# Two-layer hybrid encoder on 8 cores: casts of layer 1's mixer weights over eight steps from the fifth on, transfers of the weight sums on SyncE's queue, two of four query tiles evicted by VectorE

## The chip, the cores and the metric

The kernel runs on the 8 cores of one Trainium2 chip. Each core computes one of the 8 sequences of the batch, with the same program and the same weights; nothing passes between cores. The metric is the time on the device of the slowest core, in microseconds. The profile is that of one execution, taken on the slowest core.

## The reference

Two layers over x of shape (8, 4096, 1024), float32:

```python
for l in range(DEPTH):
    h = rmsnorm(x, norm1_g[l])
    q, k, v, r, fz, gb_in, gc_in, cx, ga, gb = split(h @ w_in[l])
    log_a = log_sigmoid(fz @ w_fg2[l] + b_fg[l]) / 16
    o = gla_chunk_causal(q * 128 ** -0.5, k, v, log_a)      # chunks of 64 frames, 4 heads
    y_a = (rmsnorm_per_head(o) * gla_norm_g[l] * silu(r)) @ w_oa[l]
    y_b = (gb_in * causal_depthwise_conv3(gc_in * cx)) @ w_ob[l]
    x = x + (sigmoid(ga) * y_a + sigmoid(gb) * y_b) @ w_o[l]
    h2 = rmsnorm(x, norm2_g[l])
    x = x + (silu(h2 @ w_gate[l]) * (h2 @ w_up[l])) @ w_down[l]   # hidden width 2816
return rmsnorm(x, final_g)
```

## The kernel before

**Steps.** A sequence of 4096 frames is cut into 8 tiles of 512. The program is a list of 24 steps: steps 0 to 7 are the mixer of layer 0 (one tile each), 8 to 11 the feed-forward part (FFN) of layer 0 (two tiles each), 12 to 19 the mixer of layer 1, 20 to 23 the FFN of layer 1. The FFN multiplies 2 by 2 blocks by Strassen's seven products, so it needs sums of weight blocks.

**Weights.** Every step streams all its weights as bf16 through a ring in SBUF (`wring`): four slots for the 20 mixer blocks of up to 1280 KB, five for FFN blocks (44 products' blocks of the gate and up weights come as 22 loads of 896 KB, `sc_gu`; 28 loads of 352 KB for the down weights, `sc_dn`). The next load is issued on SyncE's (SP's) queue by `done_block` when a slot comes free. The bf16 copies lie in DRAM and are made by the kernel itself:

- Layer 0's mixer weights are cast as they are first loaded, in steps 0 and 1, on GpSimd's (POOL's) queue.
- Layer 1's mixer weights are cast from DRAM to DRAM by 40 DMAs of `cast_piece` (L393), each half a block, issued from POOL's queue. Before: ten in each of steps 8 to 11.
- The FFN's weights of both layers go through `prep_jobs`: 66 pieces a layer. Each is loaded into `pin` (512 KB, `prep_load`, L399), POOL forms five sums and a copy in three jobs (`first`, `second`, `third`; L415 and L410), and `third` then issues the load of the next piece and the store of `pout` (448 KB, L433). Before, load and store are on POOL's queue. The pieces of layer 0 are spread over steps 2 to 7, those of layer 1 over steps 12 to 19. There is one `pin` and one `pout`, so `first` of the next piece waits until the store of this one has landed.

**Order.** Every engine runs its instructions in the order in which the program emits them. A step is a generator that yields after each group of matmuls (87 yields in a mixer step, 180 in an FFN step). After each yield the main loop also advances `sides` (norms, loads and stores of x) and pops jobs from the step's list, evenly over the yields. A job's `pace()`, and the like wait in `cast_piece`, hold POOL until TensorE (PE) has done what has been emitted so far. In a mixer step POOL also computes two small operations per unit of the linear attention, `rs2` (L751 and L753, in `C(u)`), which `E2(u)` on VectorE (DVE, L759) reads; the transposes of `Tr(u)` on PE (L768) follow.

**The start of a mixer step.** Block `fzq` gives the forget-gate code and the four query tiles in five PSUM banks. DVE copies the first (L665). The queries are scaled and evicted by ScalarE (ACT) (L674), two before and two after `gate1`, which puts eight ACT operations (four Exp, L632; four Ln, L635) between them. There are eight banks: the four groups of `v0` reuse the banks of the four queries.

Of the kernel before, what the change touches and what calls it, by code (L numbers as in the profile page):

```python
# [9 lines left out]
AF = mybir.ActivationFunctionType  # L10
ALU = mybir.AluOpType
# [24 lines left out]
class Trk:  # L36
# [56 lines left out]
    def op(self, en, R, W, f):  # L93
        e = self.E[en]
        self.deps(e, R, W)
        f(e.h).then_inc(e.sem, 1)
        e.cnt += 1
        self.record(R, W, (e.sem, e.cnt, en))
# [14 lines left out]
    def dma(self, qn, R, W, dsem, f):  # L113
        e = self.E[qn]
        self.deps(e, R, W)
        f(e.h).then_inc(dsem[0], 16)
        dsem[1] += 16
        self.record(R, W, (dsem[0], dsem[1], "dma"))
# [11 lines left out]
def _mixer_blocks():  # L130

    c = _cols()
    w = lambda n, o, k: ("w_in", c[n] + o, k)
    bl = [("fzq", 8, 640, [w("fz", 0, 16)] * 8 + [w("q", 0, 512)])]
    bl += [("v0", 8, 512, [w("v", 0, 512)])]
    bl += [("k", 8, 512, [w("k", 0, 512)])]
    bl += [("v1", 8, 512, [w("v", 512, 512)])]
    bl += [("r%d" % h, 8, 512, [w("r", h * 512, 512)]) for h in range(2)]
    bl += [("cv%d" % i, 8, 640, [w(n, i * 128, 128) for n in ("C", "X", "B", "ga", "gb")]) for i in range(8)]
    bl += [("%s%d" % (n[2:], h), 8, 512, [(n, h * 512, 512)]) for h in range(2) for n in ("w_ob", "w_oa")]  # L140
    bl += [("o%d" % h, 8, 512, [("w_o", h * 512, 512)]) for h in range(2)]
    return bl


def _ffn_blocks():

    bl = [("%s%d" % (n, p), 1, 28 * 128, None) for p in range(NPAIR) for n in ("g", "u")]
    return bl + [("d%d%s" % (n, m), 1, NPAIR * 128, None) for n in range(4) for m in PROD]
# [6 lines left out]
PH = [("mix", 0), ("ffn", 0), ("mix", 1), ("ffn", 1)]  # L155
BLOCKS = {"mix": _mixer_blocks(), "ffn": _ffn_blocks()}
# [3 lines left out]
def build_nc(S):  # L160
# [20 lines left out]
    def wblock(l, bi):  # L181
        o = sum(MIXSIZE[:bi])
        return wmix[l][o:o + MIXSIZE[bi]].rearrange("(p n) -> p n", p=128)

    with ExitStack() as es:
        tk = Trk(nc, es)
        op, mms, dma = tk.op, tk.mms, tk.dma
# [27 lines left out]
        def carve(shape, dt, mode, keys, split=False):  # L215
            n = int(np.prod(shape))
            w = n if dt == F32 else n // 2
            per = w // len(keys) if split else 0
            for i, k in enumerate(keys):
                span[k] = (mode, ao[0] + i * per, ao[0] + (i + 1) * per) if per else (mode, ao[0], ao[0] + w)  # L220
            v = (arena if dt == F32 else a16)[:, (ao[0] if dt == F32 else 2 * ao[0]):(ao[0] if dt == F32 else 2 * ao[0]) + n]
            ao[0] += w
            assert ao[0] <= AW, (mode, ao[0])
            if len(shape) == 2:
                v = v.rearrange("p (a b) -> p a b", a=shape[0])
            return v

        R2 = lambda n, a, b: [(n, i, j) for i in range(a) for j in range(b)]
        R1 = lambda n, a: [(n, i) for i in range(a)]

        qT = carve([4, T], BF16, "mix", R1("qT", 4), True)
# [12 lines left out]
        pin = carve([4, PIECE], F32, "mix", ["pin"])  # L244
        pout = carve([7, PIECE], BF16, "mix", R1("pout", 7), True)
# [43 lines left out]
        pb = [es.enter_context(nc.psum_tensor("pb%d" % i, [128, 512], F32)) for i in range(8)]  # L289
        BK = lambda i: ("bank", i)  # L290
# [5 lines left out]
        def bank():  # L296
            b = ring[0][ri[0] % len(ring[0])]
            ri[0] += 1
            return b
# [4 lines left out]
        steps = [(p, t) for p in range(4) for t in range(NT if PH[p][0] == "mix" else NT // 2)]  # L304
# [80 lines left out]
        def cast_piece(l, bi, hf):  # L385
            e = tk.E["pool"]
            tk.wait(e, tk.E["pe"].sem, tk.E["pe"].cnt)
            ds = psem[pcount[0] % NPS]
            pcount[0] += 1
            if ds[1]:  # L390
                tk.wait(e, ds[0], ds[1])
            dma("pool", [], [("scr", "mix", l, bi, hf)], ds,
                lambda q: q.dma_start(out=scr[("mix", l, bi)][64 * hf:64 * hf + 64, :], in_=wblock(l, bi)[64 * hf:64 * hf + 64, :]))  # L393

        pisem, posem = tk.newsem("pin"), tk.newsem("pout")

        def prep_load(l, i):
            dma("pool", [], ["pin"], pisem,
                lambda q: q.dma_start(out=pin, in_=wffn[l][i].rearrange("p (a b) -> p a b", a=4)))  # L399

        def prep_jobs(l):

            A12, A21, A22, A11 = (pin[:, j, :] for j in range(4))

            def pace():
                tk.wait(tk.E["pool"], tk.E["pe"].sem, tk.E["pe"].cnt)

            def total(nm, x, o, y):
                m = WSUM[nm]
                op("pool", ["pin"], [("pout", m)], lambda h: h.tensor_tensor(out=pout[:, m, :], in0=x, in1=y, op=o))  # L410

            def first():
                pace()
                op("pool", ["pin"], [("pout", 5), ("pout", 6)],
                   lambda h: h.tensor_copy(out=pout[:, 5:7, :], in_=pin[:, 2:4, :]))  # L415
                total("M1", A11, ALU.add, A22)

            def second():
                pace()
                total("M2", A21, ALU.add, A22)  # L420
                total("M5", A11, ALU.add, A12)

            def third(i):
                pace()
                total("M6", A21, ALU.subtract, A11)
                total("M7", A12, ALU.subtract, A22)
                if i + 1 < NPIECE:
                    prep_load(l, i + 1)
                if i < 2 * GQ:
                    dst = scr[("gu", l, i // 2)].rearrange("p (h a b) -> p h a b", h=2, a=7)[:, i % 2, :, :]  # L430
                else:
                    dst = scr[("dn", l)][:, :, (i - 2 * GQ) * PIECE:(i - 2 * GQ + 1) * PIECE]
                dma("pool", R1("pout", 7), [("prep", l, i)], posem, lambda q: q.dma_start(out=dst, in_=pout))  # L433

            yield lambda: prep_load(l, 0)
            for i in range(NPIECE):
                yield first
                yield second
                yield lambda i=i: third(i)
                for _ in range(5):  # L440
                    yield lambda: None
# [168 lines left out]
        def mixer(s):  # L610
            p, t = steps[s]
            l = PH[p][1]
# [54 lines left out]
            for hh in range(4):  # L667
                if hh == 2:
                    gate1()
                b = bs[1 + hh]  # L670
                if s:
                    fm_group(b, w, wk, 128 + hh * 128, h_, hk)
                op("act", [BK(b)], [("qT", hh), BK(b)],
                   lambda h, hh=hh, b=b: h.activation(out=qT[:, hh, :], in_=pb[b][:, :], func=AF.Copy, scale=128.0 ** -0.5))  # L674
                yield
            done_block(sl)

# [17 lines left out]
            for hh in range(4):  # L695
                b = bank()
                fm_group(b, w, wk, hh * 128, h_, hk)
                op("dve", [BK(b), ("dec", hh)], [("kdT", hh), BK(b)],
                   lambda h, b=b, hh=hh: h.tensor_tensor(out=kdT[:, hh, :], in0=pb[b][:, :], in1=dec[:, hh, :], op=ALU.mult))
# [182 lines left out]
            for i in range(4):  # L882
                b = bank()
# [227 lines left out]
        jobs = {}  # L1111

        def spread(fs, lo, hi):

            us = {"mix": 166.0, "ffn": 200.0}
            length = [us[PH[steps[s][0]][0]] for s in range(lo, hi)]
            ends = list(itertools.accumulate(length))
            for i, f in enumerate(fs):
                at = ends[-1] * i / len(fs)
                jobs.setdefault(lo + next(n for n, e_ in enumerate(ends) if at < e_), []).append(f)  # L1120

        NG = NT // 2
        F0, M1 = NT, NT + NG
        spread(list(prep_jobs(0)), 2, F0)
        spread([lambda bi=bi, hf=hf: cast_piece(1, bi, hf) for bi in range(len(BLOCKS["mix"])) for hf in range(2)], F0, M1)
        spread(list(prep_jobs(1)), M1, M1 + NT)

        def lead(n):
# [65 lines left out]

        GROUPS = {"mix": 87, "ffn": 180}
        RUN = {"mix": mixer, "ffn": ffn}
        for s, (p, t) in enumerate(steps):
            kind, l = PH[p]
            sg = sides(s)
            wst["kind"] = kind  # L1200
            issue_loads()
            todo = jobs.get(s, [])
            n, gi = len(todo), 0
            for _ in RUN[kind](s):
                gi += 1
                next(sg, None)
                while todo and gi * (n + 1) > GROUPS[kind] * (n - len(todo) + 1):
                    todo.pop(0)()
            for _ in sg:
                pass  # L1210
            while todo:
                todo.pop(0)()
# [79 lines left out]
```

How the kernel before makes its waits and increments, by code:

```python
    def wait(self, e, sem, val):  # L52
        if e.waited.get(id(sem), 0) < val:
            e.h.wait_ge(sem, val)
            e.waited[id(sem)] = val
# [37 lines left out]
    def op(self, en, R, W, f):  # L93
        e = self.E[en]
        self.deps(e, R, W)
        f(e.h).then_inc(e.sem, 1)
        e.cnt += 1
        self.record(R, W, (e.sem, e.cnt, en))
# [1 line left out]
    def mms(self, W, mms):  # L100
        e = self.E["pe"]
        ev = (e.sem, e.cnt + 1, "pe")
        for i, (f, R) in enumerate(mms):
            self.deps(e, R, W if i == 0 else [])
            ins = f(e.h)
            if i == len(mms) - 1:
                ins.then_inc(e.sem, 1)
                e.cnt += 1
            self.record(R, [], ev)
        self.record([], W, ev)
# [1 line left out]
    def dma(self, qn, R, W, dsem, f):  # L113
        e = self.E[qn]
        self.deps(e, R, W)
        f(e.h).then_inc(dsem[0], 16)
        dsem[1] += 16
        self.record(R, W, (dsem[0], dsem[1], "dma"))
# [332 lines left out]
        def fm_groups_kco(specs, rhsT, rkeys):  # L451
            e = tk.E["pe"]
            for kc in range(KC):
                for (b, w, wk, col0) in specs:
                    R = [wk] + rkeys(kc)
                    tk.deps(e, R, [BK(b)] if kc == 0 else [])
                    ins = e.h.matmul(pb[b][:, :], w[:, kc, col0:col0 + 128], rhsT[:, kc, :], start=(kc == 0), stop=(kc == KC - 1))
                    if kc == KC - 1:
                        ins.then_inc(e.sem, 1)
                        e.cnt += 1
                        tk.record(R, [BK(b)], (e.sem, e.cnt, "pe"))
                    else:
```

## Time and profile before

| | us |
|---|---|
| median of 3 runs | 4471.36 |
| the three runs | 4400.99, 4471.36, 4579.31 |
| the profiled execution | 4404.0 |
| its span on the slowest core | 4403.0 |
| spans of the eight cores | 4382.4 to 4403.0 |

The span lies between the first and the last instruction of the core; 1 us of the profiled execution is outside it. Over the span PE is busy for 98%, DVE for 61%, ACT for 43%, POOL for 22%. A wait is put down to what ended it. A window is a stretch of the span in microseconds from its start; a step's bounds were read off the start of its first group.

### The profile page before, as it was taken

The page shows a single profiled execution, that of the slowest core. Times are in us where ns is not written, and L with a number is a line of the kernel's source. Part 1 is how long each engine was busy: PE and PEld are TensorE (multiplying, and loading weights), DVE is VectorE, ACT ScalarE, POOL GpSimd, SP SyncE. Part 2 cuts the span into 40 slices and gives each one's busy share as a digit, 9 for nine tenths or more (in the row PEclk, how much of TensorE's full clock was granted, in tenths as well). Part 3 has the DMA queues.
Part 4 walks back from the last instruction along what each step waited for, and adds up shares of the span by engine and source line. Part 5 has one row for each costly group of instructions (what it writes and reads, how often), then busy time and mean ns, then how long its engine had stood idle before and what let it go on. Part 6 is the DMA issues. An engine that isn't in the chain of part 4 may idle for free.

```text
span 4403.0 us, 67493 instructions; the slowest of 8 cores (4382.4 to 4403.0 us)
## 1 busy us (share of the span) xinstructions
PE 4307.4 (98%) x20938; PEld 1936.8 (44%) x20938; DVE 2668.8 (61%) x4121; ACT 1877.1 (43%) x3616; POOL 973.1 (22%) x1386
## 2 busy tenths in 40 slices
PE   8999999999999999999999999999999999999998
PEld 4444444444444444444444444444444444444443
DVE  4555666666656746565555665656665666657574
ACT  3353454454443523333343544544534533435352
POOL 0002444444443000000023333323433310000000
PEclk9999999999999999999999999999999999999999
DMA  9987776776677788889786676676676665656564
GB/s 189 208 236 232 240 255 215 239 255 222 229 253 222 213 236 216 236 216 244 196 267 215 219 245 197 219 252 200 218 247 196 215 208 179 216 181 225 184 216 134
DMA packets 173997, 966.72 MB, mean 220 GB/s; under 512 B 20592, under 2 KB 20720, under 8 KB 117424
## 3 DMA queue, kind: packets, MB, share of 16 engines
q1 hardware_dynamic: 135072, 771.81, 53.6%
q0 software_dynamic: 37568, 187.98, 17.6%
q8 instruction: 177, 2.90, 0.3%
q10 hardware_dynamic: 1008, 2.62, 0.2%
q14 instruction: 172, 1.41, 0.1%
HBM read 852.75 MB, written 191.10 MB: 237 GB/s over the span
## 4 chain that ended last, share of the span: by engine, by line
PE 82%; DMA 9%; DVE 3%; ACT 3%; issue 2%; SPq 0%; ACTq 0%; DVEq 0%; POOL 0%; POOLq 0%
PE pb L445 45%; PE pb L950 32%; PE pb L457 4%; DMA sb_wring<-w_mix 3%; DMA sb_wring<-sc_gu 3%; DMA sb_wring<-sc_dn 1%; PE pb L768 1%; DMA sc_mix_cv<-sb_wring 1%; ACT sb_arena L632 1%; ACT sb_arena L635 1%; DMA sc_mix_k<-sb_wring 1%; ACT sb_sq L493 0%; DMA sb_xT<-x 0%; DMA sc_mix_r<-sb_wring 0%; DVE sb_arena L640 0%
## 5 line engine op out<-in xcount | busy, mean ns | idle before, releaser
L445 PE MATMUL pb<-sb_hT,sb_wring 128*128 128x512 bf16 x6232 | 1378.6, 380 | 8.3 <-DMA sb_wring<-w_mix 7.3
L950 PE MATMUL pb<-sb_arena,sb_wring 128*128 128x512 bf16 x5984 | 1336.3, 380 | 37.3 <-DVE pb L959 14.2
L445 PEld LDWEIGHTS pb<-sb_hT,sb_wring 128*128 128x128 bf16 x6232 | 603.8, 98 | 730.9 <-issue 33.0
L950 PEld LDWEIGHTS pb<-sb_arena,sb_wring 128*128 128x128 bf16 x5984 | 582.3, 98 | 763.3 <-issue 96.2
L962 ACT ACTIVATE sb_wring<-pb 128x512 f32<-128x512 f32 x416 | 248.3, 597 | 841.8 <-PE pb L950 816.8
L410 POOL TENSOR_TENSOR sb_arena<-sb_arena 128x256 bf16<-128x256 f32 x660 | 546.3, 850 | 98.5 <-PE pb L445 84.6
L445 PE MATMUL pb<-sb_wring,sb_hT 128*128 128x512 bf16 x2048 | 458.2, 379 | 13.0 <-ACT sb_arena L674 10.7
L445 PE MATMUL pb<-sb_arena,sb_wring 128*128 128x512 bf16 x2048 | 451.7, 380 | 7.0 <-DMA sb_wring<-w_mix 7.0
L959 DVE TENSOR_TENSOR pb<-pb,sb_wring 128x512 f32<-128x512 f32 x416 | 289.0, 695 | 234.1 <-PE pb L950 227.9
L969 DVE TENSOR_TENSOR sb_arena<-pb,sb_hT 128x512 bf16<-128x512 f32 x352 | 240.6, 690 | 230.6 <-ACT sb_wring L962 193.8
L950 PE MATMUL pb<-sb_hT,sb_wring 128*128 128x512 bf16 x1408 | 333.2, 379 | 0.1
L445 PEld LDWEIGHTS pb<-sb_arena,sb_wring 128*128 128x128 bf16 x2048 | 200.6, 98 | 250.6 <-issue 10.8
L445 PEld LDWEIGHTS pb<-sb_wring,sb_hT 128*128 128x128 bf16 x2048 | 195.8, 98 | 254.4 <-issue 28.2
L729 DVE SCALAR_TENSOR_TENSOR sb_arena<-sb_arena,sb_gam,pb 128x256 f32<-128x256 f32 x512 | 233.7, 477 | 94.5 <-PE pb L445 67.5
L415 POOL CAST sb_arena<-sb_arena 128x512 bf16<-128x512 f32 x132 | 94.7, 717 | 878.8 <-PE pb L445 533.1
L674 ACT ACTIVATE sb_arena<-pb 128x512 bf16<-128x512 f32 x64 | 37.5, 591 | 564.1 <-PE pb L445 554.6
L810 DVE SCALAR_TENSOR_TENSOR sb_arena<-sb_arena,sb_pk 128x512 f32<-128x512 f32 x256 | 210.1, 821 | 101.2 <-ACT sb_halo L804 87.1
L962 ACT ACTIVATE sb_hT<-pb 128x512 f32<-128x512 f32 x352 | 209.9, 597 | 125.4 <-PE pb L950 104.2
L457 PE MATMUL pb<-sb_arena,sb_wring 128*128 128x512 bf16 x1024 | 227.2, 379 | 1.4 <-DVE sb_arena L854 0.8
L950 PEld LDWEIGHTS pb<-sb_hT,sb_wring 128*128 128x128 bf16 x1408 | 137.5, 98 | 168.0 <-issue 3.5
L800 DVE TENSOR_TENSOR sb_arena<-pb,sb_arena 128x512 f32<-128x512 f32 x128 | 88.3, 690 | 182.8 <-PE pb L445 156.8
L803 ACT ACTIVATE sb_arena<-sb_arena,sb_pk 128x512 f32<-128x512 f32 x128 | 103.9, 812 | 208.2 <-DVE sb_arena L800 207.9
(101 smaller groups left out, 3959.6 us busy)
## 6 DMA issues: line engine op xcount, KB each, us to landing
sb_wring<-sc_gu SPq DMA_DIRECT2D x176, 896.0 KB, 6.6
sb_wring<-sc_mix_cv SPq DMA_DIRECT2D x116, 1280.0 KB, 8.0
sb_wring<-sc_dn SPq DMA_DIRECT2D x224, 352.0 KB, 3.7
sb_arena<-w_ffn POOLq DMA_DIRECT2D x132, 512.0 KB, 5.5
xs<-sb_xT SPq DMA_DIRECT2D x48, 1024.0 KB, 8.0
sb_xT<-xs SPq DMA_DIRECT2D x96, 512.0 KB, 12.4
sc_gu<-sb_arena POOLq DMA_DIRECT2D x88, 448.0 KB, 6.5
sb_wring<-sc_mix_ob SPq DMA_DIRECT2D x30, 1024.0 KB, 6.0
```

The lines of the kernel that those rows point to most:

```text
L410: op("pool", ["pin"], [("pout", m)], lambda h: h.tensor_tensor(out=pout[:, m, :], in0=x, in1=y, op=o))
L415: lambda h: h.tensor_copy(out=pout[:, 5:7, :], in_=pin[:, 2:4, :]))
L445: return lambda pe: pe.matmul(out, lhsT, rhs, start=first, stop=last)
L457: ins = e.h.matmul(pb[b][:, :], w[:, kc, col0:col0 + 128], rhsT[:, kc, :], start=(kc == 0), stop=(kc == KC - 1))
L729: lambda h, c=c, h2=h2, hh=hh: h.scalar_tensor_tensor(out=S32[1 - c][:, hh, :], in0=S32[c][:, hh, :], scalar=gam[:, hh, 2 * ts + c:2 * ts ...
L800: lambda h, b=b, u=u, csb=csb: h.tensor_tensor(out=ub[u][:, 2:T + 2], in0=pb[b][:, :], in1=csb[:], op=ALU.mult))
L803: lambda h, u=u, cc=cc, cw=cw, cacc=cacc: h.activation(out=cacc[:], in_=ub[u][:, 2:T + 2], func=AF.Identity, scale=cw(2), bias=pkc(80 + l ...
L810: lambda h, j=j: h.scalar_tensor_tensor(out=cacc[:], in0=ub[u][:, j:T + j], scalar=cw(j), in1=cacc[:], op0=ALU.mult, op1=ALU.add))
L950: fs.append((lambda pe, r=r, k=k: pe.matmul(pb[b][:, :], lhsT(k), r, start=(k == 0 and not onto), stop=(k == n - 1), skip_group_check=onto ...
L959: lambda h: h.tensor_tensor(out=pb[bo][:, :], in0=pb[b][:, :], in1=s_, op=alu))
L962: op("act", [], [BK(b), k], lambda h: h.activation(out=t_, in_=pb[b][:, :], func=func))
L969: op("dve", [("gt", i)], [BK(b), k], lambda h: h.tensor_tensor(out=out, in0=pb[b][:, :], in1=gt[i], op=ALU.mult))
```

## The change

Three things are changed.

1. The 40 casts of layer 1's mixer weights are spread over steps 4 to 11 and not 8 to 11. In steps 4 to 7 they share the job list with `prep_jobs(0)`, and the list is now sorted by each job's due time. With 166 us put down for a mixer step and 200 for an FFN step, that is a cast every 36.6 us of planned time: 5, 5, 4 and 5 in steps 4 to 7 and 5, 6, 5 and 5 in steps 8 to 11.
2. The load of `pin` and the store of `pout` of `prep_jobs` are issued on SP's queue, in both layers. The waits that come with them (on the sums, on POOL) move there too.
3. The query tiles 2 and 3 are evicted by DVE (`tensor_scalar`, times 128 ** -0.5) and not by ACT, in all 16 mixer steps.

```diff
         def prep_load(l, i):
-            dma("pool", [], ["pin"], pisem,
+            dma("sp", [], ["pin"], pisem,
...
-                dma("pool", R1("pout", 7), [("prep", l, i)], posem, lambda q: q.dma_start(out=dst, in_=pout))
+                dma("sp", R1("pout", 7), [("prep", l, i)], posem, lambda q: q.dma_start(out=dst, in_=pout))
...
-                op("act", [BK(b)], [("qT", hh), BK(b)],
-                   lambda h, hh=hh, b=b: h.activation(out=qT[:, hh, :], in_=pb[b][:, :], func=AF.Copy, scale=128.0 ** -0.5))
+                if hh < 2:
+                    op("act", [BK(b)], [("qT", hh), BK(b)],
+                       lambda h, hh=hh, b=b: h.activation(out=qT[:, hh, :], in_=pb[b][:, :], func=AF.Copy, scale=128.0 ** -0.5))
+                else:
+                    op("dve", [BK(b)], [("qT", hh), BK(b)],
+                       lambda h, hh=hh, b=b: h.tensor_scalar(out=qT[:, hh, :], in0=pb[b][:, :], scalar1=128.0 ** -0.5, scalar2=None, op0=ALU.mult))
...
-                jobs.setdefault(lo + next(n for n, e_ in enumerate(ends) if at < e_), []).append(f)
+                jobs.setdefault(lo + next(n for n, e_ in enumerate(ends) if at < e_), []).append((sum(us[PH[steps[s][0]][0]] for s in range(lo)) + at, f))
...
-        spread([lambda bi=bi, hf=hf: cast_piece(1, bi, hf) for bi in range(len(BLOCKS["mix"])) for hf in range(2)], F0, M1)
+        spread([lambda bi=bi, hf=hf: cast_piece(1, bi, hf) for bi in range(len(BLOCKS["mix"])) for hf in range(2)], 4, M1)
...
-            todo = jobs.get(s, [])
+            todo = [f for at, f in sorted(jobs.get(s, []), key=lambda a: a[0])]
```

## Rows read from the trace of the kernel before

**Rows 1.** The page: span, and PE's busy time, share and instructions.

```profile
span 4403.0 us, 67493 instructions; the slowest of 8 cores (4382.4 to 4403.0 us)
...
PE 4307.4 (98%) x20938; PEld 1936.8 (44%) x20938; DVE 2668.8 (61%) x4121; ACT 1877.1 (43%) x3616; POOL 973.1 (22%) x1386
```

**Rows 2.** Windows by step: length, busy PE PEld DVE ACT (POOL), clock, DMA share, GB/s.

```profile
1395.00:1605.00 210.00, 203.02 (x927) 90.11 (x925) 124.59 (x189) 80.66 (x132) 4.95 (x10) 0.99 0.81 223
1605.00:1815.00 210.00, 202.94 (x929) 90.43 (x927) 117.11 (x177) 71.50 (x122) 4.92 (x10) 0.99 0.86 225
1815.00:2023.00 208.00, 201.69 (x926) 90.49 (x925) 116.80 (x176) 71.55 (x122) 4.92 (x10) 0.99 0.87 227
2023.00:2224.00 201.00, 197.37 (x903) 88.34 (x901) 116.52 (x177) 77.64 (x128) 4.86 (x10) 0.99 0.82 219
3560.00:3765.00 205.00, 202.17 (x930) 90.06 (x928) 130.43 (x199) 88.28 (x146) 0.00 (x0) 1.00 0.59 193
...
887.00:1054.00 167.00, 165.82 (x838) 74.40 (x837) 105.37 (x162) 77.81 (x159) 73.86 (x104) 1.00 0.71 237
```

**Rows 3.** Waits of PE in 1395:2224 (steps 8 to 11): us, times, longest.

```profile
PE pb L950 <- DMA sb_wring<-sc_gu: 11.8, 8, 2.5
PE pb L950 <- DMA sb_wring<-sc_dn: 8.0, 5, 3.4
PE pb L950 <- DVE pb L959: 2.3, 2, 1.4
```

**Rows 4.** Waits of PE in 3560:4175 (steps 20 to 22).

```profile
PE pb L950 <- DVE pb L959: 7.3, 8, 1.5
```

**Rows 5.** DMA in 1395:2224, then in 3560:4175: queue's share; size, us to landing.

```profile
q0 software_dynamic: 1568, 23.33, 18.8%
...
sb_wring<-sc_gu SPq DMA_DIRECT2D x84, 896.0 KB, 15.3
...
sb_wring<-sc_gu SPq DMA_DIRECT2D x66, 896.0 KB, 5.0
```

**Rows 6.** Timeline of POOL in step 8: the last of its ten casts.

```profile
1534.84 0.49 POOL L393 DMA_DIRECT2D sc_mix_r<-w_mix  x1 [14.19 <-PE pb L950]
```

**Rows 7.** Who waited for L674 (the queries), and for L699: us, times.

```profile
  PE pb L445: 10.7, 15
...
  PE pb L653: 3.9, 8
```

**Rows 8.** Timelines of PE, ACT and DVE at the start of step 15.

```profile
2742.27 3.61 PE L445 MATMUL pb<-sb_wring,sb_hT 128*128 128x512 bf16 x16 [0.55 <-ACT sb_arena L674]
...
2741.55 0.58 ACT L674 ACTIVATE sb_arena<-pb 128x512 bf16<-128x512 f32 x1
...
2740.10 0.69 DVE L688 CAST sb_arena<-pb 128x512 bf16<-128x512 f32 x1 [9.12 <-PE pb L445]
```

**Rows 9.** Timelines of step 5, 948 to 971: POOL, DVE, PE, then SP.

```profile
948.16 0.55 POOL L433 DMA_DIRECT2D sc_gu<-sb_arena  x1
...
959.43 0.61 POOL L415 CAST sb_arena<-sb_arena 128x512 bf16<-128x512 f32 x1 [8.84 <-DMA sc_gu<-sb_arena]
...
962.53 0.70 POOL L753 TENSOR_TENSOR sb_rs<-sb_rs,sb_mhalf 128x2 f32<-128x2 f32 x1
...
965.47 1.06 DVE L759 SCALAR_TENSOR_TENSOR sb_arena<-pb,sb_rs,sb_arena 128x256 bf16<-128x256 f32 x2
...
970.46 0.40 PE L768 MATMUL pb<-sb_ident,sb_arena 128*128 128x128 bf16 x4
...
969.95 0.32 SPq L344 DMA_DIRECT2D sb_wring<-sc_mix_cv  x1
```

**Rows 10.** The load of block cv3 in step 5, and its landing; the landing of that store.

```profile
L344 SPq DMA_DIRECT2D sb_wring<-sc_mix_cv x1: 327/327/327, 942.1 to 942.1; - x1
...
DMA to landing us min/median/max: 19.8/19.8/19.8
...
DMA to landing us min/median/max: 11.1/11.1/11.1
```

## The prediction, made before the changed kernel was run

> **What bounds the kernel now.** I read the page first, for the engine that sets the end: TensorE is busy for 4307.4 of 4403.0 us [rows 1], at a granted clock of 0.99 to 1.00 in every window shown [rows 2]. No matmul is taken away or added by this change, so it can only act on the 95.6 us in which PE is idle. That is 2.2% of the span, and nothing can bring a gain above it.
>
> Then I laid windows over the steps, to find where the idle time lies. Length minus PE's busy time gives 7.0, 7.1, 6.3 and 3.6 us for the four FFN steps of layer 0, 24.0 in all, and 2.8 us for a step of layer 1's FFN, which does the same work [rows 2]. A mixer step idles 1.2 us. The rest of the 95.6 us is in the two first steps and the end, where the first weights and x arrive; nothing is changed there.
>
> Third, the waits of PE, stretch by stretch, for who ends the gaps. In steps 8 to 11 it is weight loads: 11.8 us on gate and up blocks, 8.0 on down blocks, and 2.3 on VectorE's additions into PSUM [rows 3]. In steps 20 to 22 only the additions are left, at 7.3 us or 2.4 a step [rows 4]. So where a load is late, the small wait behind it vanishes; one may not count both. In the mixer the query evictions end 10.7 us of PE's waits over the 16 steps, and the tile before the transposes of the keys another 3.9 [rows 7].
>
> **The casts, part 1.** Only the FFN steps of layer 0 carry them. The DMA engines are busy for 0.81 to 0.87 there and for 0.59 in layer 1 [rows 2], and a gate or up block needs 15.3 us to land where it needs 5.0 without casts [rows 5]. Casts are 18.8% of 16 engines over 829 us, or 156 us for 40: 3.9 us of all DMA engines for one. Removing 19 of 40 from these steps frees 74 us, 18.5 a step, and takes the share from about 0.84 to about 0.75.
>
> Jobs are popped evenly over 180 yields, and most of the yields lie in the gate and up part. Ten casts therefore stood some 13 to 14 us apart, with the tenth at 1534.84 [rows 6], just ahead of the down blocks, whose wait of 3.4 us is the longest one [rows 3]. With five the last falls where the ninth was and the spacing is some 25 us. The other stalls come at the end of the loads of x, where a backlog has built up; there two to three casts fewer are 8 to 12 us less backlog, against stalls of 2.5 us at most. I therefore let nearly all of it go. The ceiling is 24.0 less four times 2.8, or 12.8 us, because the waits on VectorE come back. The floor is half of that, 6, if stalls fall only as the casts do. I take 11, nearer the ceiling, as stalls need the backlog to reach a threshold.
>
> In steps 4 to 7 the casts are new: 19 of them, 74 us of DMA time over 668, so the share goes from 0.71 to about 0.82. The cover is the ring. The block with the least slack is the fourth convolution block, loaded behind 2 MB of x: issued at 942.1, landed 19.8 us later at 961.9 [rows 10], needed when the block before it is done, at 969.95 [rows 9]. That is 8 us of slack; one cast in this stretch takes 3.9, and the piece's transfers ahead of it in one queue at most 3 more, so about 1 is left. I cost this at 1 us in all, between 0 and 8 (2 us in each of four steps, should all of the cover go). Each cast also keeps POOL for 0.49 us [rows 6], which is nothing at POOL's load.
>
> **Queries by VectorE, part 3.** In step 15 PE stands for 0.55 us before the third group of `v0` until ACT has evicted query 2, begun at 2741.55 behind the eight operations of `gate1`; VectorE at that time has been idle for 9.12 us and starts on its next eviction at 2740.10 [rows 8]. Both query groups are computed before that eviction's group, so two evictions of 0.69 us (priced by that row: PSUM, 128x512, f32 to bf16) fit in the idle stretch, and the bank is free over 2 us earlier. ACT sheds two of about 0.59 us, so the key-decay chain, which goes over both engines, starts no later. The 10.7 us of [rows 7] go. The floor is 5, if PE meets the transposes' wait instead; the ceiling is 10.7 + 3.9 = 14.6. I take 10.
>
> **Transfers of the sums on SP's queue, part 2.** It moves 132 loads and 132 stores. POOL is freed of about 0.6 us for each, at a point where nothing waits for POOL: gain 0. Two things are put on SP instead. First, SP stands in `third` until POOL has formed the last sums; weight loads emitted later wait behind it. POOL works for 73.86 us of a 167 us step [rows 2], so it is mostly waiting for PE's pace and not behind it, and a weight load emitted after that has to wait for a later matmul group anyway. I estimate 0 to 2 us a load, against the 8 of slack above: nothing.
>
> Second, the store now lies in the same queue as the weights and x. The case that counts is once in each of steps 2 to 7, right behind x. The store issued at 948.16 [rows 9] landed in 11.1 us [rows 10], while the weight load issued 6 us before it, on the other queue, landed only at 961.9: it overtook. Behind that load it will land between 963 (same bytes, in order) and 967 (961.9 plus 5 for the two transfers). `first` of the next piece, at 959.43, waited for just this store. It comes 3.5 to 7.5 us later, and with it the two small operations behind the sums on POOL, done at 963.2. They would be done at 966.7 to 970.7, where VectorE wanted them at 965.47 and PE its transposes at 970.46 [rows 9]. VectorE needs 1.06, so PE's stall is 0 to 1.3 us, in ten steps perhaps: the six of layer 0, and some four of layer 1, where the pieces fall otherwise. Where a cast falls in that stretch too (steps 5 and 7) add 3.9: up to 5.2. Bounds for this part 0 and 8 x 1.3 + 2 x 5.2 = 21; I take 4, as most cases lie inside the slack.
>
> The Trainium skill (DMA: Bandwidth & Descriptors, section Queues, rings and completion order) says that each DMA engine takes turns between the queue rows that have work, so a transfer in a row of its own does not queue behind another's. The overtaking above agrees. The same page (section Issuing engines are not separate DMA queues) says that all queues share the 16 engines and interleave; by that alone this part would be 0 and not +4, the sum 4 us lower.
>
> **Sum.** -11 + 1 - 10 + 4 = -16 us: span 4403 - 16 = 4387, and with the 1 us outside it **4388 us**, 0.4% less than the profiled execution's 4404.0. The best is -12.8 - 14.6, or 4377; the worst is -6 + 8 - 5 + 21 = +18, or 4422. The three runs shown are 4401, 4471 and 4579; the profiled execution stands with the lowest, 1.5% under the median. The sum is against that execution; a median taken over runs that scatter so could read up to 4471 - 16 = 4455 and a little more for the same program.
>
> **The rivals.**
> - **The store turns into the new wait.** The late store, as above, at its upper end: ten stalls come to 12 to 21 us and eat the gain. -11 + 1 - 10 and these give -8 to +1, say 4401. For it: this store already ends an 8.84 us idle of POOL [rows 9], so there is no room left. Against it: 4 to 7 us of slack between POOL, VectorE and PE.
> - **Little moves.** The casts still collide in the FFN and the query wait only moves to the next bank or to the transposes: -6 - 5 + 5, or 4398. For it: the small waits that reappear [rows 4]. Against it: five casts leave the down blocks alone.
> - **Slower by over 2%.** In-order waiting locks SP and POOL together: SP holds weight loads for POOL's sums, POOL's `first` waits for a store behind those loads, and each piece, not one a step, comes late. It decides from where a store lands over 8 us after `first` is due for most pieces; then the attention's operations hold VectorE, four banks are not enough, and each of the 14 steps with pieces loses 8 us: 112 - 21, or 4495. Against it: the weights' slack is 8 us at the least and DMA is busy for 0.71 only [rows 2].
> - **Faster by over 2%** would need nearly all idle time; nothing here does that.
>
> **How the numbers follow.** Forecast 0.62; little moves 0.14; the store's wait 0.19; slower by over 2% 0.04; faster by over 2% 0.01. 2% is about what a measurement of this kernel can tell from no change. So faster 0.01, same 0.95, slower 0.04. The forecast's own range is 4377 to 4400. For 8 in 10 it reaches over the rivals at 4398 and 4401 and, as the shown runs scatter upwards alone, to where such a median could be: 4372 to 4470.
>
> **What would show it.** The FFN steps of layer 0 at about 205 us with gate and up blocks landing in 7 to 10 us and under 4 us of waits on them; no wait of PE on L674; one wait of `first` per step on the store, of 11 to 15 us; mixer steps 4 to 7 at 167 us. Wrong: PE waiting on `rs2`'s readers (L759, L800) by several us in steps 2 to 7, waits on `sc_mix` loads in 4 to 7, or FFN steps still at 209.

## The result

The changed kernel takes 0.9939 of the time of the one before (95% interval 0.9915 to 0.9963), some 27 us of 4400. By the bound of 2% that is no change, though this interval leaves out 1; measured again later (e12), the same kernel gave 0.9969 (0.9924 to 1.0014), which does not. The profiled execution took 4372.67 us, against 4404.0. (The medians over all runs, 4487.73 and 4436.17 us, say nothing here: in some executions of either kernel one or both dies ran at a lower granted clock, and the ratio leaves these out, as the table of steps below does.)

In the changed kernel's trace L954, L963, L979, L763, L772 and L703 are the lines L950, L959, L975, L759, L768 and L699 of before. The page, span and first line of engines, to be laid beside [rows 1]:

```profile
span 4371.6 us, 67989 instructions; the slowest of 8 cores (4353.4 to 4371.6 us)
...
PE 4297.7 (98%) x20938; PEld 1937.1 (44%) x20938; DVE 2692.2 (62%) x4153; ACT 1862.6 (43%) x3584; POOL 817.3 (19%) x1122
```

The matmuls are as many as before; PE idles for 73.9 us instead of 95.6. Windows over steps 8 to 11, step 20 and steps 4 and 5 (columns as in [rows 2]):

```profile
1397.00:1602.00 205.00, 200.96 (x925) 89.69 (x924) 124.54 (x189) 80.68 (x132) 2.46 (x5) 1.00 0.75 222
1602.00:1802.00 200.00, 199.77 (x926) 90.26 (x925) 116.65 (x177) 71.56 (x122) 2.95 (x6) 1.00 0.76 224
1802.00:2002.00 200.00, 199.77 (x927) 90.39 (x926) 116.79 (x177) 71.57 (x122) 2.43 (x5) 1.00 0.71 217
2002.00:2200.00 198.00, 196.17 (x905) 88.24 (x903) 116.94 (x179) 77.66 (x128) 2.43 (x5) 1.00 0.67 207
3529.00:3734.00 205.00, 202.19 (x930) 90.31 (x929) 130.99 (x199) 88.28 (x146) 0.00 (x0) 1.00 0.59 193
717.00:887.00 170.00, 168.17 (x840) 75.25 (x839) 106.59 (x165) 77.00 (x157) 63.91 (x87) 0.99 0.81 247
887.00:1057.00 170.00, 166.22 (x837) 74.54 (x836) 108.56 (x163) 76.69 (x157) 66.28 (x86) 1.00 0.78 247
```

Steps 9 and 10 idle for 0.2 us each and last 200 us. That is 5 us less than layer 1's step, which I had taken for the floor. The DMA share fell to 0.67 to 0.76. Mixer steps 4 and 5 carry casts now, at a share of 0.78 to 0.81, and last 170 instead of 167 us on this core. Waits of PE in 1397:2200, to be laid beside [rows 3]; then gate and up loads and the casts' queue in the same stretch, beside [rows 5]:

```profile
PE pb L954 <- DVE pb L963: 2.3, 2, 1.4
PE pb L954 <- DMA sb_wring<-sc_dn: 1.3, 1, 1.3
PE pb L954 <- DMA sb_wring<-sc_gu: 1.2, 1, 1.2
```

```profile
q0 software_dynamic: 859, 12.74, 9.3%
...
sb_wring<-sc_gu SPq DMA_DIRECT2D x84, 896.0 KB, 6.7
```

Weight waits fell from 19.8 to 2.5 us, while the waits on VectorE did not come back. A gate or up block lands in 6.7 us, not 15.3. Waits of PE in steps 4 to 7 (720:1396), then in step 2 (380:552):

```profile
PE pb L772 <- DVE sb_arena L763: 3.6, 5, 1.4
PE pb L653 <- DVE sb_arena L703: 2.1, 3, 1.0
...
PE pb L772 <- DVE sb_arena L763: 3.8, 2, 3.5
```

No wait on the queries is left. What is new is PE waiting for the attention's output, L763: the rival's place. Every profiled execution was then split at its steps' bounds on every core, and the lengths averaged over the cores, or over those named (us; e5 and e11 stand further down):

| | steps 0, 1 | 2, 3 | 4 to 7 | 8 to 11 | 12 to 19 |
|---|---|---|---|---|---|
| before | 382.8 | 333.9 | 675.8 | 822.8 | 1336.4 |
| changed | 375.7 | 335.8 | 676.4 | 802.9 | 1329.7 |
| e1 queries alone | 376.2 | 331.9 | 670.3 | 821.5 | 1330.9 |
| e2 casts alone | 379.1 | 334.0 | 695.5 | 803.2 | 1336.4 |
| e3 sums on SP alone (cores 0 to 3) | 378.8 | 341.1 | 675.2 | 822.5 | 1336.7 |
| e4 changed without SP | 379.0 | 332.1 | 697.8 | 803.0 | 1330.9 |
| e6 only the store on SP | 377.8 | 338.3 | 709.7 | 805.7 | 1330.9 |
| e7 only the load on SP (cores 4 to 7) | 379.6 | 345.7 | 702.5 | 804.0 | 1331.0 |
| e8 casts from step 6 | 377.6 | 337.1 | 681.6 | 802.8 | 1329.4 |
| e9 casts 12 and 28 | 378.0 | 334.9 | 673.1 | 802.3 | 1329.8 |
| e10 and early pieces on POOL | 379.1 | 333.0 | 676.3 | 801.9 | 1329.7 |
| e12 changed again (cores 4 to 7) | 376.1 | 337.5 | 682.1 | 801.6 | 1329.3 |

Steps 20 to 23 take 842.2 before and 842.4 after. The mean span fell by 31.1: 7.1 in steps 0 and 1, 19.9 in 8 to 11, 6.7 in 12 to 19, less 2.5 lost in 2 to 7. Steps 0 and 1 are no measure: there casts alone and sums alone, which touch nothing in them, also read 4 us less.

### The profile page after: what moved, and what is told of

It reads as the page before. It is cut to its first block, busy times and chain, and to the rows that moved or that the text cites. A ratio compares the mean times of both kernels' runs of the same rounds, so it can differ in the third digit from the quotient of the medians.

```text
span 4371.6 us, 67989 instructions; the slowest of 8 cores (4353.4 to 4371.6 us)
## 1 busy us (share of the span) xinstructions
PE 4297.7 (98%) x20938; PEld 1937.1 (44%) x20938; DVE 2692.2 (62%) x4153; ACT 1862.6 (43%) x3584; POOL 817.3 (19%) x1122
## 3 DMA queue, kind: packets, MB, share of 16 engines
q1 hardware_dynamic: 206880, 901.59, 62.5%
## 4 chain that ended last, share of the span: by engine, by line
PE 85%; DMA 9%; DVE 2%; issue 1%; ACT 1%; POOL 1%; SPq 0%; ACTq 0%; DVEq 0%; POOLq 0%
PE pb L445 45%; PE pb L954 34%; PE pb L457 4%; DMA sb_wring<-w_mix 3%; DMA sc_dn<-sb_arena 1%; DMA sc_mix_cv<-sb_wring 1%; DMA sc_gu<-sb_arena 1%; PE pb L772 1%; POOL sb_arena L410 1%; DMA sb_wring<-sc_mix_fzq 1%; DMA sc_mix_k<-sb_wring 0%; DMA sb_xT<-x 0%; DVE sb_arena L973 0%; DMA sb_wring<-sc_gu 0%; DMA sc_mix_ob<-sb_wring 0%
## 5 line engine op out<-in xcount | busy, mean ns | idle before, releaser
L954 PE MATMUL pb<-sb_arena,sb_wring 128*128 128x512 bf16 x5984 | 1328.0, 379 | 19.7 <-DVE pb L963 14.4
L954 PEld LDWEIGHTS pb<-sb_arena,sb_wring 128*128 128x128 bf16 x5984 | 581.9, 98 | 737.7 <-issue 63.1
L963 DVE TENSOR_TENSOR pb<-pb,sb_wring 128x512 f32<-128x512 f32 x416 | 289.1, 695 | 212.1 <-PE pb L954 205.3
L954 PE MATMUL pb<-sb_hT,sb_wring 128*128 128x512 bf16 x1408 | 333.2, 379 | 0.1
L675 ACT ACTIVATE sb_arena<-pb 128x512 bf16<-128x512 f32 x32 | 19.0, 597 | 562.2 <-PE pb L445 552.7
L954 PEld LDWEIGHTS pb<-sb_hT,sb_wring 128*128 128x128 bf16 x1408 | 137.5, 98 | 168.0 <-issue 3.5
```

What stands on the lines that cost most here:

```text
L954: fs.append((lambda pe, r=r, k=k: pe.matmul(pb[b][:, :], lhsT(k), r, start=(k == 0 and not onto), stop=(k == n - 1), skip_group_check=onto ...
L963: lambda h: h.tensor_tensor(out=pb[bo][:, :], in0=pb[b][:, :], in1=s_, op=alu))
```

## The experiments

**e1, e2, e3: each part alone**, on the kernel before. The diff of e1 is that of `hh < 2`, of e2 that of `spread`, the due times and `sorted`, of e3:

```diff
-            dma("pool", [], ["pin"], pisem,
+            dma("sp", [], ["pin"], pisem,
...
-                dma("pool", R1("pout", 7), [("prep", l, i)], posem, ...
+                dma("sp", R1("pout", 7), [("prep", l, i)], posem, ...
```

> The kernel before with the third part alone: query tiles 2 and 3 evicted by VectorE. My theory: PE's waits on the query evictions go (10.7 us over 16 steps, 0.5 to 0.6 us in each mixer step), and the wait before the key transposes (3.9 us) goes partly, as ScalarE has less in front of the key decay; 10 to 15 us off the span. Rival: the wait moves to the next bank or to the transposes, and less than 5 us go.

Measured: one execution at 4385.9 us beside 17 of before at 4397 to 4436. Steps 2 to 7 and 12 to 19 are 13.0 us shorter together. Waits of PE in steps 2 to 7 (380:1390):

```profile
PE pb L457 <- DVE sb_arena L858: 1.0, 2, 0.8
PE pb L653 <- DVE sb_arena L703: 0.8, 2, 0.5
```

The wait on the queries is gone, and the one of the key transposes shrank with it, from 2.9 us in these steps (L699 before) to 0.8. The theory holds.

> The kernel before with the first part alone: casts over steps 4 to 11. My theory before the result put the gain in the FFN of layer 0 at 11 us, with layer 1's FFN step as the floor of a step. The changed kernel showed about 200 us in steps 9 and 10, under layer 1's 205; so now 18 to 22 us over steps 8 to 11. Steps 4 to 7 lose 0 to 1 us each. Rival: part of what steps 8 to 11 gained in the changed kernel comes from another part, and here they gain 11 us or less.

Measured: ratio 1.0002 (0.9978 to 1.0026). The FFN of layer 0 gains 19.6 us, as expected of this part alone. Steps 4 to 7 lose 19.7, and here both theories missed. Timelines of step 7 in e2, in the order POOL, VectorE, PE, and PE's waits in 719:1400:

```profile
1262.40 0.73 POOL L393 DMA_DIRECT2D sc_mix_cv<-w_mix  x1
...
1288.41 0.95 POOL L433 DMA_DIRECT2D sc_dn<-sb_arena  x1
...
1304.60 0.61 POOL L415 CAST sb_arena<-sb_arena 128x512 bf16<-128x512 f32 x1 [14.11 <-DMA sc_dn<-sb_arena]
...
1310.56 0.77 POOL L393 DMA_DIRECT2D sc_mix_cv<-w_mix  x1
...
1311.74 0.72 POOL L753 TENSOR_TENSOR sb_rs<-sb_rs,sb_mhalf 128x2 f32<-128x2 f32 x1
...
1312.63 1.07 DVE L759 SCALAR_TENSOR_TENSOR sb_arena<-pb,sb_rs,sb_arena 128x256 bf16<-128x256 f32 x2 [13.91 <-POOL sb_rs L753]
...
1313.37 0.85 PE L768 MATMUL pb<-sb_ident,sb_arena 128*128 128x128 bf16 x4 [7.88 <-DVE sb_arena L759]
...
PE pb L768 <- DVE sb_arena L759: 16.1, 6, 7.9
```

The store issued at 1288.41 lands 16.1 us later. `first` waits for it, the sums come next, then `rs2`; VectorE stands for 13.91 us and PE for 7.88. This is the chain that the prediction drew, but with the sums on POOL's queue, in a kernel in which the prediction had put 1 us. The store does not stand behind a cast: the one before it, of 1262.40, landed after 9.6 us, and the next is issued at 1310.56. Beside it a load of h (1024 KB) and two convolution blocks are under way. What the casts change is not this one landing but the pace of all pieces; it is measured behind e7.

> The kernel before with the second part alone: load and store of the weight sums on SyncE's queue. Theory: the store behind x lands 3 to 7 us later, the small operations of the attention on GpSimd follow it late, and PE waits for VectorE's output of the attention (L759) for 1 to 4 us in some of steps 2 to 7; 4 to 12 us slower than before in all, with almost nothing of it in steps 12 to 19. Rival: nothing moves (0 to 2 us), because all queues share the same 16 engines.

Measured: ratio 1.0000 (0.9972 to 1.0028). Steps 2 and 3 lose 7 us, in step 2 alone; 4 to 7 and 12 to 19 lose nothing. The ratio cannot tell 7 us from none; the steps can. The mechanism was right in one step of six.

**e4: the changed kernel without part 2.**

```diff
-            dma("sp", [], ["pin"], pisem,
+            dma("pool", [], ["pin"], pisem,
...
-                dma("sp", R1("pout", 7), ...
+                dma("pool", R1("pout", 7), ...
```

> The changed kernel with the load and the store of the weight sums back on GpSimd's queue (parts 1 and 3 alone). Theory: steps 2 to 7 lose their waits on L763 and come to 166 us each, 5 to 10 us less than in the changed kernel; steps 8 to 19 as in the changed kernel. Rival: the casts in steps 4 to 7 are what costs there, and taking the sums off SyncE's queue gives nothing, or something is lost, since GpSimd now issues all of them.

Measured: ratio 0.9971 (0.9940 to 1.0002). Steps 2 and 3 gain 3.7 us, but 4 to 7 lose 21.4 against the changed kernel. The rival came about, not the theory: part 2, which alone costs 7 us, carries the casts in the mixer. Waits of VectorE on `rs2` in steps 4 to 7, in e4 and then in the changed kernel:

```profile
DVE sb_arena L763 <- POOL sb_rs L757: 53.6, 13, 14.0
```

```profile
DVE sb_arena L763 <- POOL sb_rs L757: 22.5, 8, 5.7
```

**e5: by which way does it reach PE?** e4 without the two operations of `rs2`: `E2` scales by `ss[r]`.

```diff
-                    op("pool", [("ss", r, h2) for h2 in range(2)], [("rs2", r)], ...
-                    op("pool", [("rs2", r), "mhalf"], [("rs2", r)], ...
...
-                               scalar=rs2[r][:, h2:h2 + 1], ...
+                               scalar=ss[r][:, h2:h2 + 1], ...
```

> e4_without_sp with the two small operations of the attention on GpSimd (rs2) left out: VectorE scales by the plain sum of squares, so the per-head norm is not computed. Everything else, casts, sums and their queue included, stays. Theory: GpSimd is late because store and load of the sums lie behind a cast in its queue, and the lateness reaches TensorE only through rs2; so steps 4 to 7, 697.8 us in e4 as the mean of the cores, come to 670 to 674. Rival: the casts slow the weight loads and x themselves, and steps 4 to 7 stay over 690.

Measured: steps 4 to 7 take 672.5 us (mean of cores 4 to 7), 25 less, at a DMA share of 0.85 to 0.87 against 0.79 to 0.82 in e4. Windows of steps 6 and 7 on core 6, and the one wait of PE on another engine in its steps 4 to 7:

```profile
1047.00:1212.00 165.00, 164.00 (x820) 74.43 (x834) 106.39 (x163) 76.56 (x157) 68.35 (x90) 1.00 0.86 252
1212.00:1383.00 171.00, 169.95 (x849) 77.12 (x863) 103.94 (x162) 69.48 (x149) 73.87 (x95) 1.00 0.85 257
...
PE pb L445 <- DVE sb_arena L733: 0.4, 1, 0.4
```

The casts slow neither weights nor x enough to matter. Of the 27.5 us that e4 loses against e1 (670.3), 25.3 go by way of two operations of 0.2 and 0.7 us that stand behind the sums in POOL's order.

**e6, e7: store alone, load alone on SP's queue**, on e4: one of the two lines of e3's diff each.

> e4_without_sp with the store of the sums alone on SyncE's queue, the load left on GpSimd's. Theory: in e4 what is waited for is the store behind a cast, so most of the 20 us lost in steps 4 to 7 come back (676 to 682 us for the four), but the load behind a cast still costs something. Rival: the load behind the cast is what makes the next piece late, and the four steps stay over 690.

> e4_without_sp with the load of the sums' pieces alone on SyncE's queue, the store left on GpSimd's. Theory: the store still lands behind the cast, steps 4 to 7 stay at 688 to 698 us. Rival: the load was what counted, and they come to 680 or less.

Measured: 709.7 and 702.5 us in steps 4 to 7, both worse than e4's 697.8. In e6 the rival's time came about (over 690), in e7 the theory's direction, 4.5 us beyond its range: neither transfer is the culprit alone. POOL's waits in 720:1390 in e6, with the load's median landing (5.4 us before), and in e7 (at a granted clock of 0.98 to 0.99):

```profile
POOL sb_arena L415 <- DMA sb_arena<-w_ffn: 234.5, 29, 12.9
...
sb_arena<-w_ffn POOLq DMA_DIRECT2D x41, 512.0 KB, 9.6
```

```profile
POOL sb_arena L415 <- DMA sc_gu<-sb_arena: 134.9, 19, 10.3
POOL sb_arena L415 <- DMA sc_dn<-sb_arena: 115.5, 14, 12.5
```

**Is it the casts' queue?** `first` waits for both transfers, so a piece takes POOL a cycle of two parts: from `first` to the end of the last sum, and from there until load and store have both landed. Means over the pieces of steps 4 to 7, on the same cores as above, read from the issues and landings in the traces (us):

| | sums | to both landed | cycle | steps 4 to 7 |
|---|---|---|---|---|
| e3 sums on SP alone | 5.4 | 7.3 | 12.7 | 675.2 |
| e9 casts 12 and 28 | 5.3 | 8.0 | 13.3 | 673.1 |
| before | 5.2 | 8.8 | 14.0 | 675.8 |
| e1 queries alone | 5.2 | 8.9 | 14.1 | 670.3 |
| changed | 5.4 | 8.9 | 14.3 | 676.4 |
| e2 casts alone | 5.2 | 10.3 | 15.5 | 695.5 |
| e4 changed without SP | 5.1 | 10.4 | 15.5 | 697.8 |
| e5 e4 without `rs2` | 4.8 | 10.7 | 15.5 | 672.5 |
| e7 only the load on SP | 5.1 | 10.5 | 15.6 | 702.5 |
| e6 only the store on SP | 5.1 | 10.6 | 15.7 | 709.7 |

The schedule has 11 pieces in a step of 166 us, one every 15.1. The kernels whose cycle is under that lose 0 to 6 us against before or e1; those above it fall behind and lose 20 to 39, but for e5, in which nothing on VectorE waits for POOL. The casts add 1.5 us to a cycle that had 1.1 us of room. Part 2 takes 1.2 to 1.3 us off, with casts or without: the store is issued 0.5 us after the last sum and not 1.2, and both land sooner.

It takes off as much where no cast is near. A piece with a cast still on its way when its store is issued needs 12.5 us to both landings in e4, one that meets no cast 9.6; in the changed kernel, where the casts have POOL's queue to themselves, 10.1 and 7.7. So leaving the casts' queue does not spare the sums the casts: 2.9 us become 2.4. A transfer of the sums left on POOL's queue without the other is slow even without a cast in flight: in e6 such loads take 9.0 us on average, in e4 6.7. Why, was not settled. That the excess over 15.1 us makes the loss is read from this order of ten kernels; no run changed the pace of the pieces alone.

**e8: how many casts does a step bear?**

```diff
-        spread([... cast_piece(1, bi, hf) ...], 4, M1)
+        spread([... cast_piece(1, bi, hf) ...], 6, M1)
```

> The changed kernel with the casts over steps 6 to 11 and not 4 to 11: 12 in steps 6 and 7, seven in each FFN step where the changed kernel has five or six and the one before ten. Theory of a threshold (stalls only from a backlog on): the FFN steps stay within 1 to 2 us of the changed kernel's (802.9 us for the four), and steps 4 and 5 gain 3 us together. Rival, stalls in proportion to the casts: the four FFN steps lose a third of the 20 us gained, 809 to 811.

Measured: ratio 0.9943 (0.9910 to 0.9976). FFN steps with seven casts take 802.8 us, as with five or six: a threshold, which lies between seven and ten. Steps 4 and 5 gain 5 us, but 6 and 7, with six casts each, lose 10. Waits of PE in 1052:1405:

```profile
PE pb L772 <- DVE sb_arena L763: 10.7, 4, 7.7
```

**e9, e10: a version drawn from this.** e9 divides the casts otherwise; e10 also puts the first 21 pieces back on POOL's queue, with semaphores of their own.

```diff
-        spread([... cast_piece(1, bi, hf) ...], 4, M1)
+        casts = [... cast_piece(1, bi, hf) ...]
+        spread(casts[:12], 4, F0)
+        spread(casts[12:], F0, M1)
```

> The changed kernel with the 40 casts divided otherwise: 12 over steps 4 to 7 (three each) and 28 over steps 8 to 11 (seven each). Theory: three casts in a mixer step leave the store of the sums in time, so steps 4 to 7 come to 670 to 673 us against 676.4 of the changed kernel, and seven in an FFN step still cost nothing (802 to 804 for the four): 3 to 6 us faster. Rival: the few casts that are left still meet the store behind x, and nothing moves.

> As e9, and the transfers of the first 21 pieces (steps 2 and 3, where no cast runs) back on GpSimd's queue. Theory: the wait on the attention in step 2 goes, steps 2 and 3 come to 332 us as with the queries alone, against 335.8; 3 us faster than e9. Rival: they stay at 335 or more.

> The changed kernel itself, on the same chip as e9 and e10, as their measure. Expected: 0.993 to 0.995 of the kernel before, steps 4 to 7 at 675 to 678 us, 8 to 11 at 802 to 804.

Measured: e9 0.9929 (0.9906 to 0.9951), e10 0.9944 (0.9902 to 0.9986), the changed kernel again 0.9969 (0.9924 to 1.0014). In e9 steps 4 to 7 come to 673.1, 3 to 9 us under the changed kernel's executions. Its waits of PE in 720:1394:

```profile
PE pb L772 <- DVE sb_arena L763: 3.3, 4, 1.9
```

e10 saves 2 us in steps 2 and 3, and its steps 4 to 7 read 3 us more than e9's. The wait that it was to end is still there on its slowest core, 3.8 us in step 2. The changed kernel itself read 676.4 and 682.1 in steps 4 to 7, and 682.2 in e11, which is the same program up to there; the second is beyond the 675 to 678 expected. So 6 us lie between executions, and e8's 681.6 as a whole shows no loss; its steps 6 and 7 do, at 350.2 us against 340.3 to 344.0. e9 has the lowest ratio, but the intervals overlap: not shown to be better than the changed kernel.

**e11: what is the floor of an FFN step?** The changed kernel without squares, sum and scaling of the final norm.

```diff
-                if l == DEPTH - 1:
-                    squares.append((hf, dc))
...
-            op("dve", [("xT", hf, kc), key, "pk"], [("xT", hf, kc)], ... scalar_tensor_tensor ...
```

> The changed kernel with the final norm left out: x goes out as it is, without the squares, their sum and the scaling on VectorE. It tells what a FFN step costs without any neighbour. Theory: steps 20 to 22 fall from 205 us to the 199.8 that steps 9 and 10 of the changed kernel take, and the waits on the additions into PSUM (2.6 us a step) go, so these waits come from the final norm's work on VectorE and were no floor for layer 0. Rival: they stay at 204 to 205, and layer 0's FFN is faster for another reason.

Measured, windows over steps 20, 21 and 22:

```profile
3545.00:3750.00 205.00, 202.18 (x930) 90.33 (x929) 124.66 (x190) 80.64 (x132) 0.00 (x0) 1.00 0.60 194
3750.00:3950.00 200.00, 199.77 (x926) 90.28 (x925) 116.67 (x177) 71.67 (x122) 0.00 (x0) 1.00 0.62 204
3950.00:4150.00 200.00, 199.77 (x926) 90.37 (x925) 116.82 (x177) 71.57 (x122) 0.00 (x0) 1.00 0.63 206
```

Steps 21 and 22 last 200 us with 0.2 idle, as steps 9 and 10 of the changed kernel do; there the theory holds. Step 20 does not fall: 205 us with 2.8 idle, 2.3 of them waits on the additions. It is the first FFN step of its layer, as step 8 is, which takes 205 us in the changed kernel.

## Why the prediction was right, and where not

The range (4372 to 4470) and the direction held; -16 us stood for what measured -27, and -14 in e12. The sum was nearer than its steps: too little for the FFN and too little for the loss in steps 2 to 7 partly cancel, and that is luck.

- **FFN of layer 0: -11 forecast, -19.9 measured.** The right part: gate and up blocks land in 6.7 us, and the fifth cast leaves the down blocks alone. The failed step is the ceiling, "24.0 less four times 2.8, or 12.8 us, because the waits on VectorE come back". I took layer 1's step for the floor of all four. Its steps carry the final norm on VectorE, 133.64 us in step 21 against 117.11 in step 9 of the kernel before, and e11 shows that the 5 us between steps 21 and 22 and steps 9 and 10 are this. Step 20, the one in [rows 2], stays at 205 us in e11, so the norm is not its reason; step 8, also the first of its layer, takes 205 too, but 9 and 10 do not. A second term was missing. After a weight wait of 2.54 us the granted clock fell in the kernel before. Its window of step 21, then PE's timeline and windows around that wait:

```profile
3765.00:3970.00 205.00, 202.16 (x929) 90.47 (x928) 133.64 (x207) 87.33 (x146) 0.00 (x0) 1.00 0.61 200
...
1680.00 5.30 PE L950 MATMUL pb<-sb_arena,sb_wring 128*128 128x512 bf16 x16 [2.54 <-DMA sb_wring<-sc_gu]
...
1680.00:1681.10 1.10, 1.10 (x6) 0.51 (x7) 0.00 (x0) 0.00 (x0) 0.00 (x0) 1.00 0.71 216
1681.10:1684.50 3.40, 3.40 (x10) 1.20 (x9) 0.86 (x2) 0.60 (x1) 0.00 (x0) 0.50 0.95 270
1684.50:1690.00 5.50, 5.50 (x27) 2.54 (x26) 4.39 (x8) 2.88 (x5) 0.00 (x0) 1.00 0.96 237
```

  0.50 is the level of 1.2 GHz of the two. For 3.4 us the work goes at half speed, so 1.7 us are lost beside the wait. Steps 8 to 11 had 18 such stretches on the eight cores before, three of them twice as long, and one after: 4.3 us less lost per core. With the idle time, which fell by 14.6 (mean of the cores), that makes 18.9 of the 19.9. The rest is open.
- **Queries: -10 forecast, about -13 measured** over 14 steps (e1), inside the bounds of 5 and 14.6. VectorE's evictions take 0.692 us, and the first starts 5 us before ACT's used to in its step. What I held back for, a wait of PE at the transposes instead, did not come: ACT, freed of two evictions, brings the key decay forward, by 0.8 us in step 15.
- **Casts in steps 4 to 7: +1 forecast.** True of what I argued from, weights and their slack: no wait on a `sc_mix` load in these steps. The failed step is what "I cost this at 1 us in all" leaves out: it asks whether the weights have slack (8 us) and not whether POOL's pieces have. Their cycle had 1.1 us of room in 15.1, and the casts add 1.5. Without part 2 this costs 19.7 us (e2).
- **Sums on SP's queue: +4 forecast, for a transfer that comes to stand behind x.** It happens, in step 2. The changed kernel's POOL and PE there, and the landing of the two stores in 440:470:

```profile
461.50 0.61 POOL L415 CAST sb_arena<-sb_arena 128x512 bf16<-128x512 f32 x1 [15.99 <-DMA sc_gu<-sb_arena]
...
466.01 0.27 PE L772 MATMUL pb<-sb_ident,sb_arena 128*128 128x128 bf16 x2 [3.51 <-DVE sb_arena L763]
...
DMA to landing us min/median/max: 4.7/10.6/16.5
```

  Against e1, the changed kernel loses 3.9 us in steps 2 and 3 and 6.1 in 4 to 7. That is 10 us for my +1 and +4, the mechanism right and its size half. In steps 12 to 19 it loses nothing (e3). I had the wrong sign for the part as a whole: beside the casts it costs 3.7 us in steps 2 and 3 and is worth 21.4 in 4 to 7. The failed step is "at a point where nothing waits for POOL: gain 0". `first` of the next piece waits for what is issued there, and the move shortens its cycle by 1.2 to 1.3 us, for which there is no use alone (e3) and much beside the casts. I priced the parts one by one and added; they aren't additive.
- **The page's rules.** The Trainium skill (DMA: Bandwidth & Descriptors, section Queues, rings and completion order) has each DMA engine take turns between queue rows. I used it for what the store loses by leaving POOL's row. That it would gain by leaving a row that casts fill is not borne out as a cause here: a cast in flight costs a piece 2.9 us in its own row (e4) and 2.4 in another (changed kernel). That all queues share the same 16 engines (section Issuing engines are not separate DMA queues) is no ground for a price of 0: e4 and the changed kernel move the same bytes, and differ by 21.4 us in steps 4 to 7.
- **The rivals.** The store as new wait came about, at 10 us and not 12 to 21. Slower by 2% did not: even in e6, the worst, the lateness cost 39 us in four steps and stayed out of steps 12 to 19. "Little moves" is refuted by e1 and e2 (13.0 us from the queries, 19.6 in the FFN).

## What to carry to other kernels

Before work is added beside a helper engine's jobs, measure their cycle, work and landing together, against the time that the schedule leaves them: here 14.0 of 15.1 us. Below that limit a microsecond more or less is worth little, above it each one counts on every piece, so two edits that meet in one cycle have to be priced together: here the casts alone were worth 0 over steps 2 to 19, the transfers alone 7 us lost, and both, on top of the queries, 10 us gained. A neighbouring stage is a floor only if every engine does the same in it: compare the other engines' busy time in the two windows first, for more than the stage's first step. And a small operation on a loaded helper engine is a path from that engine's DMA waits into the main one.

## What the runs showed of the hardware

- A piece's load of 512 KB and store of 448 KB had both landed 9.6 us after the sums with no cast about and 12.5 with one in flight in the same queue (e4), 7.7 and 10.1 with the casts in another (changed kernel). With the store moved to the other queue, the load landed in a median of 9.6 us instead of 5.4 (e6).
- PE's granted clock fell to the half level around waits: for 3.4 us after one of 2.54, which so cost 4.2, and for 10.2 us from within the stop of 7.88 us in e2, of which 6.1 lay behind it.
- The same bytes are cut into more packets on SP's queue. The page of the changed kernel, queue rows (before: 135072 packets of 771.81 MB and 37568 of 187.98 MB):

```profile
q1 hardware_dynamic: 206880, 901.59, 62.5%
q0 software_dynamic: 5888, 58.20, 8.4%
```

  71808 packets more on the one and 31680 fewer on the other, for 130 MB. The share of DMA time did not rise: 62.5 and 8.4% together, against 53.6 and 17.6%.
